# Moving the last dense product of a streaming encoder among the gathered expert rows

## The chip, the cores and the metric

One core of a Trainium2 chip runs the whole kernel. The metric is the device time of one execution in microseconds, as the median of several runs. Everything is float32.

## The reference, cut to what matters

One layer of a streaming encoder works on 576 tokens (512 of a prompt, 64 of a sample) of width 2048. A token mixer comes first, then the PEER channel mixer: each token picks 128 experts out of 16,384; row `u[idx]` of each gives a dot product with the token, and row `v[idx]` is added to the token with a weight made from it. The last step is the one that is changed here:

```python
h = h + _peer(_rmsnorm(h, g_ffn), ...)
e = _rmsnorm(h, g_ple)
h = h + jax.nn.sigmoid(e @ w_ple_gate) * (p @ w_ple_proj)
y = _rmsnorm(h, g_final)
```

`w_ple_gate` is 2048x2048, `w_ple_proj` is 256x2048.

## The kernel before

Tokens are five blocks of 128: blocks 0 to 3 are the prompt, block 4 (`SB`) holds the 64 sample tokens twice, each half with half of the experts. Blocks 0, 3 and 4 get their experts by gathers, one row of 128x2048 numbers (1 MB, one expert for each of 128 tokens) at a time; blocks 1 and 2 (`DENSE`) get only the `u` rows so, and their `v` part by a dense product of 32 steps (`NVG`), each with 4 MB of `peer_v` tiles. There are 576 `u` rows (`NROWS`); the `v` rows of a block follow their `u` rows 12 rows later (`LAG`). Rows 512 to 575 belong to block 4.

GpSimd issues the gathers into a ring of slots, six of them at the end (three for `u`, three for `v`), each when VectorE has used the slot's last row. VectorE works a `u` row at L2282 (`dots`) and a `v` row at L2294. ScalarE applies a GELU once in eight `u` rows (L1752, after rows 535, 543, 551, 559, 567, 575), and VectorE multiplies it with the gate before the first `v` row of those eight.

The embedding stage (`pe_embed`, `act_embed`, `dve_embed`) does the last step for blocks 1, 2, 3 and 0 (`EMBEDS[0]`, four blocks). First the blocks are turned: a quarter of a block is four 128x128 transposes on TensorE (L834) into one PSUM bank, which ScalarE copies with the gain (L842). ScalarE squares each block (L1320), VectorE and ScalarE make 1/rms of it (L848, L1323, L851; `dve_rs`, `act_rs`). Then come four groups of 512 columns (`DG`); in each, TensorE multiplies the four blocks with a 4 MB piece of `w_ple_gate`, loaded as four quarters (L1242, SyncE issues at L667), and with a piece of `w_ple_proj` (L1250); ScalarE takes the sigmoid (L1681); VectorE takes the result in two steps, `sigmoid * proj` (L2192) and the addition to h (L2196). Block 0 has been kept in memory (`h_scratch`) and is read back at L712, after the last dense step. The embedding of block 4 itself (`pe_last`, L1267 to L1296, and `sp_last`, which loads `w_ple_gate` once more as 16 rows of 1 MB, `w_row`) follows when all its rows are added, and then the final norm.

Each engine runs its instructions in one fixed order. It is written down as a key: every program yields numbers on a common scale, whose unit is one `u` row, and `braid` merges the programs by them. A `v` row has the key of the `u` row before it plus 0.5. So `EMBED_AT = (533, 1.05)` puts the turned copies of ScalarE at 534.05 to 535.0 and the four norms at 535.3 to 537, and `GROUP_ROWS = (538, 11.9)` puts what VectorE and ScalarE do for group i at 538 + 11.9 i. Equal keys go to the gathered rows first. TensorE and SyncE do these stages in plain program order.

Of the kernel before, what the change touches and what calls it, by code (L numbers as in the profile page):

```python
# [10 lines left out]
ALU = mybir.AluOpType  # L11
ACT = mybir.ActivationFunctionType
# [3 lines left out]
D = 2048  # L16
# [5 lines left out]
EPS = 1e-6  # L22
# [54 lines left out]
DENSE_AT = (404.6, 4.0)  # L77
GROUP_ROWS = (538, 11.9)

# [278 lines left out]
def build(nc, a, out):  # L358
    with ExitStack() as ctx:
# [159 lines left out]
        pT = late[:, 2 * D - NB * PLE:2 * D].rearrange("p (k t) -> p k t", k=PK)  # L519
        sig = late[:, 0:D].rearrange("p (i c) -> p i c", i=4)  # L520

        def hrow(t):

            return X[:, 4 * D:5 * D] if t == 0 else hslot(t)
        Wf = W[:, :, :].rearrange("p k c -> p (k c)")
# [8 lines left out]
        h2, sig2 = hslot(SB)[:, 0:2 * CG], hslot(SB)[:, 2 * CG:4 * CG]  # L534
        gf2 = late[:, 0:2 * CG]

# [42 lines left out]
        def ncol(i, c):  # L579
            return stat[:, 4 * i + c:4 * i + c + 1]  # L580

        def rs_of(what, g, j):
# [124 lines left out]
        def sp_embed(sp):  # L707
            sp.wait_ge(d_done, 4 * (NVG - 1))
            load_w(sp, a["w_ple_gate"][0], "ple", 0, range(0, 1))
            sp.wait_ge(d_done, 4 * NVG)  # L710
            sp.wait_ge(h_kept, 16)
            sp.dma_start(hrow(0), h_keep).then_inc(h_in, 16)  # L712
            for k in range(PK):
                sp.dma_start(wp[:, k, :], a["w_ple_proj"][0, k * P:(k + 1) * P, :]).then_inc(wp_in, 16)
            load_w(sp, a["w_ple_gate"][0], "ple", 0, range(1, DG))

        def sp_last(sp):

            for k in range(KT):
                if k < WQ - 1:  # L720
                    sp.wait_ge(used[k], prod.use0["ple", 0] + DG)
                elif k == WQ - 1:
                    sp.wait_ge(mm, prod.end("ple", 0))
                elif k == WQ:
                    sp.wait_ge(v_used, v_rows(NROWS) - 6)
                    sp.dma_start(cx[:, :], a["g_final"].rearrange("(o d) -> o d", o=1).to_broadcast([P, D])).then_inc(gf_in, 16)
                elif 6 <= k < 12:
                    _, what, x = ends[k - 6]
                    if what == "u":
                        sp.wait_ge(u_used, x + 1)  # L730
                    else:
                        sp.wait_ge(v_used, v_rows(x) + 1)
                elif k >= 12:
                    sp.wait_ge(row_used, k - 11)
                sp.dma_start(w_row(k), a["w_ple_gate"][0, k * P:(k + 1) * P, :]).then_inc(row_landed(k)[0], 16)
            sp.wait_ge(y_ready, y0 + 1)
            sp.dma_start(every_second(out["y_sample"][0], 0), halves(h2)[0].rearrange("p (a c) -> p a c", c=CG)).then_inc(y_out, 16)
# [15 lines left out]
        def sp_dense(sp):  # L753
# [12 lines left out]
            for m in range(NVG):  # L766
                if m * VT % CHUNK == 0:
                    c = m * VT // CHUNK
                    if c >= 2:
                        sp.wait_ge(d_done, 4 * (m - 2))  # L770
                    sp.dma_start(a_chunk(c).rearrange("p t k -> p (t k)"), a_keep[c].rearrange("i t k -> i (t k)")
                                 ).then_inc(chunk_in[c % 2], 16)
                if m == NVG - 4:
                    sp.wait_ge(picked[SB], PAIRS)
                    load_p(sp)
                if m >= 2:
                    sp.wait_ge(d_done, 4 * (m - 1))
                if m:
                    load_tiles(sp, m)

        def sync(sp):
# [55 lines left out]
        def act_turned(act, what, g, q, j, n, gain, src_bank):  # L837
# [5 lines left out]
            ins.then_inc(n_cp, 1)  # L843

        def dve_rs(dve, i, at, x):
            yield at(x)
            dve.wait_ge(n_sq, i + 1)
            dve.tensor_scalar(ncol(i, 1), ncol(i, 0), 1.0 / D, EPS, ALU.mult, ALU.add).then_inc(n_ms, 1)  # L848
            yield at(x + 0.1)
            dve.wait_ge(n_rt, i + 1)  # L850
            dve.reciprocal(ncol(i, 3), ncol(i, 2)).then_inc(n_rs, 1)  # L851
# [367 lines left out]
        def pe_embed(pe):  # L1219
            ts, n = EMBEDS[0], len(EMBEDS[0])  # L1220
            pe.wait_ge(d_add, 4 * NVG)
            for q in range(4):
                for j, t in enumerate(ts):
                    x = q * n + j
                    if x >= 6:
                        pe.wait_ge(n_cp, counts.quarter0["ple", 0] + x - 5)
                    if q == 0 and t == 3:
                        pe.wait_ge(v_used, v_rows(ROW0[SB]))
                    if q == 0 and t == 0:
                        pe.wait_ge(h_in, 16)  # L1230
                    pe_turn(pe, "ple", 0, q, j, n, hrow(t), x % 6)
            pe.wait_ge(n_cp, counts.quarters("ple", 0))
            pe.wait_ge(p_c, 2)
            for i in range(DG):
                U = prod.use0["ple", 0] + i
                for q in range(WQ):
                    pe.wait_ge(landed[q], 16 * (U + 1))
                    for j in range(n):
                        if q == 0 and i:
                            pe.wait_ge(e_sig, (i - 1) * n + j + 1)  # L1240
                        for k in range(q * KQ, (q + 1) * KQ):
                            ins = pe.matmul(bank(j), aT(k, j), W[:, k, :], start=(k == 0), stop=(k == KT - 1))  # L1242
# [10 lines left out]
                    if q < WQ - 1:  # L1253
                        ins.then_inc(used[q], 1)

        def pe_last(pe):
# [61 lines left out]
        def act_rs(act, i, src, junk, at, x):  # L1318
            yield at(x)
            act.activation(junk, src, ACT.Square, accum_out=ncol(i, 0)).then_inc(n_sq, 1)  # L1320
            yield at(x + 0.05)
            act.wait_ge(n_ms, i + 1)
            act.activation(ncol(i, 2), ncol(i, 1), ACT.Sqrt).then_inc(n_rt, 1)  # L1323
# [334 lines left out]
        def act_embed(act):  # L1658
# [4 lines left out]
            for q in range(4):  # L1663
                for j in range(n):
                    yield at(1 + 0.3 * q)
                    act_turned(act, "ple", 0, q, j, n, 2, (q * n + j) % 6)
            for j, t in enumerate(ts):
                i = counts.stat["ple", 0, j]
                if j:
                    act.wait_ge(n_sq, i)  # L1670
                yield from act_rs(act, i, hrow(t), late[:, 0:D], at, 2.2 + 0.5 * j)
            for i in range(DG):
                for j in range(n):
                    x = i * n + j
                    yield group_at(i, 0.3 * j)
                    act.wait_ge(mm, prod.mm0["ple", 0] + x + 1)
                    if i == 0:
                        act.wait_ge(n_rs, counts.stat["ple", 0, j] + 1)
                    if x >= 4:
# [3 lines left out]
        def act_last(act):  # L1683

            i, junk = counts.stat["ple", 1, 0], psum[:, 2:6, :].rearrange("p b c -> p (b c)")
            ts, squares = EMBEDS[0], late[:, 0:D]
            yield last_at(0)
# [29 lines left out]
            for s in range(2):  # L1717
                yield last_at(5 + s)
                act.wait_ge(n_rs, i + 1)
                act.wait_ge(mm, prod.end("ple", 0) + s + 1)  # L1720
# [458 lines left out]
        def dve_embed(dve):  # L2179
            ts, n = EMBEDS[0], len(EMBEDS[0])  # L2180

            def at(x):
                return embed_at(0, x)
            for j in range(n):
                yield from dve_rs(dve, counts.stat["ple", 0, j], at, 2.22 + 0.5 * j)
            for i in range(DG):
# [145 lines left out]
```

## Time and profile before

| | |
|---|---|
| time, median of 3 runs | 3743.24 us (3733.95 to 3745.58) |
| profiled execution, first to last instruction (span) | 3741.8 us; its time outside the span is not recorded, and the median is 1.4 us above the span |
| TensorE busy | 3104.3 us, 83% |
| VectorE busy | 2756.7 us, 74% |
| GpSimd busy | 1354.3 us, 36% |
| ScalarE busy | 624.2 us, 17% |
| DMA over the span | 388 GB/s mean; 417 to 422 GB/s in most slices |
| slice 37 of 40 (about 3368 to 3461 us) | 206 GB/s |
| chain that ended last | DMA 45%, VectorE 17%, TensorE 12% |

The busy shares are means over stages with different limits, so they say little about one stage. The change touches the last tenth of the span, and the views of that stretch are the ones to read.

### The profile page before, as it was taken

What the parts mean: (1) busy time and instruction counts of PE and PEld (TensorE: products, weight loads), DVE (VectorE), ACT (ScalarE), POOL (GpSimd) and SP (SyncE); (2) the same over time, 40 slices, a digit from 0 to 9 for tenths busy, and PEclk for the clock granted to TensorE, in tenths of its full rate; (3) what the DMA queues carried; (4) which work ended last, traced back from release to release, by engine and by line L of the source; (5) the groups of instructions that cost most, each with busy time, mean ns of one, the idle gap of its engine ahead of it and who ended that gap; (6) DMA issues with size and microseconds to landing.
All of it is one profiled execution on the core that took longest, in us unless ns stands there. A gap on an engine that the chain in (4) does not pass through costs nothing.

```text
span 3741.8 us, 26599 instructions
## 1 busy us (share of the span) xinstructions
PE 3104.3 (83%) x9234; PEld 1897.2 (51%) x9234; DVE 2756.7 (74%) x3844; ACT 624.2 (17%) x1601; POOL 1354.3 (36%) x908
## 2 busy tenths in 40 slices
PE   8998697999977299998886444999889999869974
PEld 4447343544456144554366433766666666644432
DVE  1014988677677899878768888888788998774885
ACT  2211110132011121123121556000000000002012
POOL 0001543325235453323335432334333433352662
PEclk9999798999988599999898556999999999989997
DMA  8889999999999999999999999999999999995998
GB/s 267 280 278 328 419 417 418 418 418 419 417 412 405 357 418 417 417 418 380 395 405 413 348 361 336 422 421 422 422 421 421 419 422 399 404 418 206 414 420 342
DMA packets 310262, 1453.01 MB, mean 388 GB/s; under 512 B 25776, under 2 KB 64112, under 8 KB 172016
## 3 DMA queue, kind: packets, MB, share of 16 engines
q0 software_dynamic: 129840, 944.83, 61.7%
q1 hardware_dynamic: 170112, 493.78, 34.6%
q10 hardware_dynamic: 10176, 12.70, 0.9%
q8 instruction: 73, 1.20, 0.1%
q14 instruction: 61, 0.50, 0.0%
HBM read 1424.48 MB, written 26.74 MB: 388 GB/s over the span
## 4 chain that ended last, share of the span: by engine, by line
DMA 45%; DVE 17%; PE 12%; POOL 6%; issue 6%; ACT 2%; SPq 0%; DVEq 0%; POOLq 0%; ACTq 0%
DMA ring<-in_peer_v,eidx 18%; DMA ring<-in_peer_u,eidx 17%; DVE ring L2282 7%; POOL ring L827 6%; PE psum L891 6%; DMA W<-in_w_peer_q 5%; DVE arena L2294 3%; DMA W<-in_w_out 2%; PE psum L1242 2%; PE psum L1154 1%; DMA a_scratch<-arena 1%; PE psum L1204 1%; DMA a_scratch<-W 1%; DMA arena<-h_scratch 1%; PE psum L1287 1%
## 5 line engine op out<-in xcount | busy, mean ns | idle before, releaser
L2282 DVE CUSTOM_DVE_ANT_0 ring<-ring,cx 128x2048 f32<-128x2048 f32 x576 | 1313.8, 2286 | 256.4 <-DMA ring<-in_peer_u,eidx 254.1
L827 POOL DMA_INDIRECT ring<-in_peer_u,eidx x576 | 868.9, 1509 | 1635.5 <-DVE dots L2282 1210.5
L2294 DVE SCALAR_TENSOR_TENSOR arena<-ring,wts,arena 128x2048 f32<-128x2048 f32 x320 | 751.7, 2349 | 210.6 <-DMA ring<-in_peer_v,eidx 192.4
L891 PE MATMUL psum<-W,actT 128*128 128x512 f32 x1792 | 797.4, 604 | 46.7 <-ACT actT L842 21.8
L827 POOL DMA_INDIRECT ring<-in_peer_v,eidx x320 | 480.3, 1501 | 665.9 <-DVE arena L2294 619.7
L891 PEld LDWEIGHTS psum<-W,actT 128*128 128x128 f32 x1792 | 343.9, 194 | 467.1 <-issue 450.6
L1154 PE MATMUL psum<-actT,W 128*128 128x128 f32 (+2 forms) x1536 | 294.9, 358 | 90.1 <-DMA W<-in_w_peer_q 79.2
L1154 PEld LDWEIGHTS psum<-actT,W 128*128 128x128 f32 x1536 | 269.3, 212 | 114.8 <-DMA W<-in_w_peer_q 86.0
L1752 ACT ACTIVATE gel<-dots 128x8 f32<-128x8 f32 x72 | 15.6, 216 | 1630.0 <-DVE dots L2282 1630.0
L1204 PE MATMUL psum<-arena 128*128 128x512 f32 x512 | 236.3, 619 | 38.4 <-DVE arena L2177 38.4
L1204 PE MATMUL psum<-arena,actT 128*128 128x512 f32 x512 | 233.2, 612 | 27.7 <-DVE arena L2177 27.5
L891 PE MATMUL psum<-W,arena 128*128 128x512 f32 x512 | 227.6, 606 | 23.9 <-DMA W<-in_w_out 23.6
L1204 PE MATMUL psum<-W,actT 128*128 128x512 f32 x512 | 225.4, 600 | 19.4 <-DMA actT<-a_scratch 16.1
L1204 PE MATMUL psum<-W,arena 128*128 128x512 f32 x512 | 225.8, 601 | 9.3 <-DVE arena L2177 9.1
L1204 PEld LDWEIGHTS psum<-arena 128*128 128x128 f32 x512 | 159.5, 316 | 114.6 <-DVE arena L2177 47.1
L1204 PEld LDWEIGHTS psum<-arena,actT 128*128 128x128 f32 x512 | 159.3, 315 | 100.3 <-DVE arena L2177 32.2
L1204 PEld LDWEIGHTS psum<-W,actT 128*128 128x128 f32 x512 | 159.9, 314 | 83.6 <-issue 20.5
L869 PE MATMUL psum<-W,actT 128*128 128x512 f32 x448 | 197.5, 600 | 0.0
L1204 PEld LDWEIGHTS psum<-W,arena 128*128 128x128 f32 x512 | 159.8, 314 | 74.3 <-DVE arena L2177 10.5
L891 PEld LDWEIGHTS psum<-W,arena 128*128 128x128 f32 x512 | 98.6, 195 | 148.8 <-issue 118.7
L2177 DVE TENSOR_TENSOR arena<-psum,arena 128x1024 f32<-128x1024 f32 x128 | 155.7, 1217 | 0.0
L869 PEld LDWEIGHTS psum<-W,actT 128*128 128x128 f32 x448 | 85.3, 193 | 102.3 <-issue 102.0
(317 smaller groups left out, 2558.0 us busy)
## 6 DMA issues: line engine op xcount, KB each, us to landing
W<-in_w_in SPq DMA_DIRECT2D x168, 1024.0 KB, 12.4
W<-in_peer_v SPq DMA_DIRECT2D x64, 1024.0 KB, 15.8
arena<-in_peer_v SPq DMA_DIRECT2D x64, 1024.0 KB, 17.9
W<-in_w_out SPq DMA_DIRECT2D x48, 1024.0 KB, 17.4
W<-in_w_peer_q SPq DMA_DIRECT2D x48, 1024.0 KB, 24.2
W<-in_w_ple_gate SPq DMA_DIRECT2D x24, 1024.0 KB, 14.8
ring<-in_peer_u,eidx POOLq DMA_INDIRECT x576, 17.4
a_scratch<-W SPq DMA_DIRECT2D x8, 1024.0 KB, 14.4
```

The source lines that it names most:

```text
L827: pool.indirect_dma_start(ring[:, slot, :], None, a["peer_u" if what == "u" else "peer_v"][0], off(ix, 0)).then_inc(ring_in[slot], 16)
L869: ins = pe.matmul(bank(4 * s + j), lhs(k, j), W[:, k, :], start=(k == 0), stop=(k == KT - 1))
L891: ins = pe.matmul(bank(4 * s + j), lhs(at_k, j), w_pair(q)[:, k, s * CG:(s + 1) * CG], start=(at_k == 0), stop=(at_k == KT - 1))
L1154: ins = pe.matmul(bank(2 * (i % 2) + c // 2)[:, at:at + fresh], W[:, k, c * P:(c + 1) * P], actT[:, k, 0:fresh], start=(k == 0 and c % 2 = ...
L1204: ins = pe.matmul(bank(at % 3 * 2 + half), a_chunk(c)[:, i // 2 * P:(i // 2 + 1) * P, m * VT % CHUNK + x], v_tiles(m)[:, x, c0:c0 + 512], ...
L1242: ins = pe.matmul(bank(j), aT(k, j), W[:, k, :], start=(k == 0), stop=(k == KT - 1))
L1287: ins = pe.matmul(psum[SAMPLE * b:SAMPLE * (b + 1), s, :], actT[:, k, 0:SAMPLE], w_row(k)[:, cols_of(s, b)], start=(k == 0), stop=(k == KT ...
L1752: act.activation(gel[:, n % DEEP, :], dots[:, n % DEEP, :], ACT.Gelu).then_inc(gelud, 1)
L2177: dve.tensor_tensor(hc, psum[:, at % 3 * 2:at % 3 * 2 + 2, :], hc, ALU.add).then_inc(d_add, 1)
L2282: dve.tensor_tensor_reduce(row, row, cx[:, :], 1.0, 0.0, ALU.mult, ALU.add, dots[:, n % DEEP, c:c + 1]).then_inc(u_used, 1)
L2294: dve.scalar_tensor_tensor(out=hslot(t), in0=ring[:, slot, :], scalar=wts[:, n % DEEP, c:c + 1], in1=hslot(t), op0=ALU.mult, op1=ALU.add). ...
```

## The change

The squares of the four blocks are taken as soon as each block's last quarter is copied, and the four means, roots and reciprocals become one instruction each on 128x4 numbers (`embed_cols`), at key 541.5 (`EMBED_RS`). `rooted` adapts the counts of the semaphores to that. The keys of the groups go from 538, 549.9, 561.8, 573.7 to 548.5, 559, 569.5, 580; there is no gathered row above 575.5. Block 0 of h is read back by SyncE behind the tiles of the last dense step, into half of ring slots 6 and 7 (`late`), and the sigmoids and the squares go to the place (`spare`) where it was before. TensorE turns the first two quarters, does quarter 0 of group 0's product, turns quarter 2, does quarter 1 of the product, turns quarter 3, and goes on; turning uses banks 4 to 7 (four instead of six). In `sp_last` the load of `g_final` into `cx` moves from row 4, where it waited for all but six `v` rows, to row 6, where it waits for the last `u` row.

```diff
-GROUP_ROWS = (538, 11.9)
+GROUP_ROWS = (548.5, 10.5)
+EMBED_RS = 541.5
...
-        sig = late[:, 0:D].rearrange("p (i c) -> p i c", i=4)
+        spare = X[:, 4 * D:5 * D]
+        sig = spare.rearrange("p (i c) -> p i c", i=4)
         def hrow(t):
-            return X[:, 4 * D:5 * D] if t == 0 else hslot(t)
+            return late[:, 0:D] if t == 0 else hslot(t)
...
+        def embed_cols(c):
+            i = counts.stat["ple", 0, 0]
+            return stat[:, 4 * i:4 * (i + len(EMBEDS[0]))].rearrange("p (f c) -> p f c", c=4)[:, :, c]
...
             load_w(sp, a["w_ple_gate"][0], "ple", 0, range(0, 1))
             sp.wait_ge(d_done, 4 * NVG)
-            sp.wait_ge(h_kept, 16)
-            sp.dma_start(hrow(0), h_keep).then_inc(h_in, 16)
...
-                elif k == WQ:
-                    sp.wait_ge(v_used, v_rows(NROWS) - 6)
+                elif k == 6:
+                    sp.wait_ge(u_used, NROWS)
                     sp.dma_start(cx[:, :], a["g_final"]...)
-                elif 6 <= k < 12:
+                if 6 <= k < 12:
...
                 if m:
                     load_tiles(sp, m)
+                if m == NVG - 1:
+                    sp.wait_ge(p_t, 2)
+                    sp.wait_ge(h_kept, 16)
+                    sp.dma_start(hrow(0), h_keep).then_inc(h_in, 16)
...
+        def rooted(i):
+            return min(i, counts.stat["ple", 0, 0]) + 1 + (1 if i >= counts.stat["ple", 1, 0] else 0)
...
         def pe_embed(pe):
             ts, n = EMBEDS[0], len(EMBEDS[0])
-            pe.wait_ge(d_add, 4 * NVG)
-            for q in range(4):
+            def turn(q):
                 for j, t in enumerate(ts):
                     x = q * n + j
-                    if x >= 6:
-                        pe.wait_ge(n_cp, counts.quarter0["ple", 0] + x - 5)
+                    if x >= 4:
+                        pe.wait_ge(n_cp, counts.quarter0["ple", 0] + x - 3)
...
-                    pe_turn(pe, "ple", 0, q, j, n, hrow(t), x % 6)
-            pe.wait_ge(n_cp, counts.quarters("ple", 0))
+                    pe_turn(pe, "ple", 0, q, j, n, hrow(t), 4 + x % 4)
+            pe.wait_ge(d_add, 4 * NVG)
             pe.wait_ge(p_c, 2)
+            turn(0)
+            turn(1)
             for i in range(DG):
...
+                        if i == 0:
+                            pe.wait_ge(n_cp, counts.quarter0["ple", 0] + q * n + j + 1)
                         for k in range(q * KQ, (q + 1) * KQ):
...
+                    if i == 0 and q + 2 < 4:
+                        turn(q + 2)
...
         def act_embed(act):
             for q in range(4):
-                for j in range(n):
+                for j, t in enumerate(ts):
                     yield at(1 + 0.3 * q)
-                    act_turned(act, "ple", 0, q, j, n, 2, (q * n + j) % 6)
-            for j, t in enumerate(ts):
-                i = counts.stat["ple", 0, j]
-                if j:
-                    act.wait_ge(n_sq, i)
-                yield from act_rs(act, i, hrow(t), late[:, 0:D], at, 2.2 + 0.5 * j)
+                    act_turned(act, "ple", 0, q, j, n, 2, 4 + (q * n + j) % 4)
+                    if q < 3:
+                        continue
+                    i = counts.stat["ple", 0, j]
+                    if j:
+                        act.wait_ge(n_sq, i)
+                    act.activation(spare, hrow(t), ACT.Square, accum_out=ncol(i, 0)).then_inc(n_sq, 1)
+            yield EMBED_RS
+            act.wait_ge(n_ms, rooted(counts.stat["ple", 0, 0]))
+            act.activation(embed_cols(2), embed_cols(1), ACT.Sqrt).then_inc(n_rt, 1)
...
         def dve_embed(dve):
-            for j in range(n):
-                yield from dve_rs(dve, counts.stat["ple", 0, j], at, 2.22 + 0.5 * j)
+            yield EMBED_RS
+            dve.wait_ge(n_sq, counts.stat["ple", 0, n - 1] + 1)
+            dve.tensor_scalar(embed_cols(1), embed_cols(0), 1.0 / D, EPS, ALU.mult, ALU.add).then_inc(n_ms, 1)
+            yield EMBED_RS + 0.6
+            dve.wait_ge(n_rt, rooted(counts.stat["ple", 0, 0]))
+            dve.reciprocal(embed_cols(3), embed_cols(2)).then_inc(n_rs, 1)
```

## Rows read from the trace of the kernel before

**Rows 1.** Windows of the last stretch: busy time by engine, clock, DMA share.

```profile
core 0: us, PE busy (x) PEld busy (x) DVE busy (x) ACT busy (x) POOL busy (x), PEclk, DMA share, GB/s
3355.00:3380.00 25.00, 9.25 (x54) 7.67 (x55) 0.00 (x0) 14.75 (x54) 0.94 (x1) 0.70 0.79 328
3355.00:3450.00 95.00, 79.25 (x212) 38.52 (x213) 29.23 (x33) 28.59 (x72) 15.00 (x10) 0.90 0.56 219
...
3450.00:3657.00 207.00, 178.90 (x417) 78.99 (x415) 176.10 (x132) 16.56 (x22) 132.07 (x71) 0.94 1.01 413
```

**Rows 2.** Timeline of VectorE: start, length, line, operation, idle time before.

```profile
3352.70 2.29 DVE L2282 CUSTOM_DVE_ANT_0 ring<-ring,cx 128x2048 f32<-128x2048 f32 x1 [0.93 <-DMA ring<-in_peer_u,eidx]
...
3380.78 0.15 DVE L848 TENSOR_SCALAR stat<-stat 128x1 f32<-128x1 f32 x1 [25.78 <-ACT ring L1320]
...
3428.15 0.69 DVE L2192 TENSOR_TENSOR ring<-psum,ring 128x512 f32<-128x512 f32 x1 [31.10 <-PE psum L1250]
...
3689.26 2.35 DVE L2294 SCALAR_TENSOR_TENSOR arena<-ring,wts,arena 128x2048 f32<-128x2048 f32 x1 [2.83 <-DMA ring<-in_peer_v,eidx]
```

**Rows 3.** Timeline of TensorE from the first turn to the last product.

```profile
3339.90 2.82 PE L834 MATMUL psum<-misc,arena 128*128 128x128 f32 x12 [6.24 <-DVE arena L2177]
3364.10 6.09 PE L834 MATMUL psum<-misc,arena 128*128 128x128 f32 x40 [21.38 <-DMA arena<-h_scratch]
...
3378.81 9.75 PE L1242 MATMUL psum<-W,actT 128*128 128x512 f32 x16 [5.53 <-ACT arena L842]
...
3443.33 7.03 PE L1242 MATMUL psum<-W,actT 128*128 128x512 f32 x16
...
3627.01 1.88 PE L1250 MATMUL psum<-arena,ring 128*128 128x512 f32 x4
```

**Rows 4.** Timeline of ScalarE: turned copies, square, GELU, table load, sigmoid.

```profile
3366.26 2.19 ACT L842 ACTIVATE actT<-psum,gT 128x128 f32<-128x128 f32 x8
...
3378.33 2.33 ACT L1320 ACTIVATE ring<-arena 128x2048 f32<-128x2048 f32 x1
...
3463.15 0.21 ACT L1752 ACTIVATE gel<-dots 128x8 f32<-128x8 f32 x1 [19.35 <-DVE dots L2282]
...
3559.23 0.21 ACT L1752 ACTIVATE gel<-dots 128x8 f32<-128x8 f32 x1 [45.42 <-DVE dots L2282]
3559.46 1.28 ACT L1681 ACT_TABLE_LOAD   x1
3560.75 1.84 ACT L1681 ACTIVATE ring<-psum,stat 128x512 f32<-128x512 f32 x3
...
3657.17 0.21 ACT L1752 ACTIVATE gel<-dots 128x8 f32<-128x8 f32 x1 [27.96 <-DVE dots L2282]
```

**Rows 5.** DMA queues: packets, MB, share; 3306 to 3355 us.

```profile
q0 software_dynamic: 2229, 16.21, 80.1%
q1 hardware_dynamic: 2013, 4.02, 21.7%
```

**Rows 6.** The loads of w_ple_gate at line 667.

```profile
L667 SPq DMA_DIRECT2D W<-in_w_ple_gate x16: 367/368/9768, 3306.2 to 3565.4; - x16
...
DMA to landing us min/median/max: 5.0/16.2/51.3
```

**Rows 7.** Timeline of TensorE, and its clock, after the last gathered row.

```profile
3681.66 5.03 PE L1267 MATMUL psum<-arena,ring 128*64 128x512 f32 x16 [52.77 <-DVE arena L2294]
3691.66 7.09 PE L1272 MATMUL psum<-misc,arena 128*128 128x64 f32 x32 [4.97 <-DVE arena L2294]
3698.68 8.49 PE L1287 MATMUL psum<-W,actT 128*64 128x512 f32 x32
...
3724.51 7.04 PE L1287 MATMUL psum<-W,actT 128*64 128x512 f32 x32
...
3692.00:3696.00 4.00, 4.00 (x21) 4.00 (x20) 0.00 (x0) 1.55 (x8) 0.00 (x0) 0.50 1.01 420
```

**Rows 8.** Timeline of ScalarE's DMA queue: the writes of y_prompt.

```profile
3718.40 7.13 ACTq L1716 DMA_DIRECT2D out_y_prompt<-arena  x4
```

More of the change, by code:

```diff
@@ L534, in build @@
         h2, sig2 = hslot(SB)[:, 0:2 * CG], hslot(SB)[:, 2 * CG:4 * CG]
-        gf2 = late[:, 0:2 * CG]
+        gf2 = spare[:, 0:2 * CG]
         ends = ring_ends()
@@ L732, in sp_last @@
                         sp.wait_ge(v_used, v_rows(x) + 1)
-                elif k >= 12:
+                if k >= 12:
                     sp.wait_ge(row_used, k - 11)
@@ L849, in dve_rs @@
             yield at(x + 0.1)
-            dve.wait_ge(n_rt, i + 1)
+            dve.wait_ge(n_rt, rooted(i))
             dve.reciprocal(ncol(i, 3), ncol(i, 2)).then_inc(n_rs, 1)
@@ L1321, in act_rs @@
             yield at(x + 0.05)
-            act.wait_ge(n_ms, i + 1)
+            act.wait_ge(n_ms, rooted(i))
             act.activation(ncol(i, 2), ncol(i, 1), ACT.Sqrt).then_inc(n_rt, 1)
@@ L1676, in act_embed @@
                     act.wait_ge(mm, prod.mm0["ple", 0] + x + 1)
-                    if i == 0:
-                        act.wait_ge(n_rs, counts.stat["ple", 0, j] + 1)
+                    if x == 0:
+                        act.wait_ge(n_rs, rooted(counts.stat["ple", 0, 0]))
                     if x >= 4:
@@ L1685, in act_last @@
             i, junk = counts.stat["ple", 1, 0], psum[:, 2:6, :].rearrange("p b c -> p (b c)")
-            ts, squares = EMBEDS[0], late[:, 0:D]
+            ts, squares = EMBEDS[0], spare
             yield last_at(0)
@@ L1718, in act_last @@
                 yield last_at(5 + s)
-                act.wait_ge(n_rs, i + 1)
+                act.wait_ge(n_rs, rooted(i))
                 act.wait_ge(mm, prod.end("ple", 0) + s + 1)
```

## The prediction

> **What bounds the kernel now.** I read the page first, for which stretch is ill: in nearly every slice DMA is full and slice 37 falls to 206 GB/s. Then windows around it [rows 1]: from 3450 to 3657 us DMA is 100% busy at 413 GB/s while VectorE is busy 176 of 207 us, so the gathered rows are bound by DMA there. From 3355 to 3450 DMA moves only 219 GB/s. At the 413 of the later window, the same bytes take 50 us: 45 us of the 95 are lost. VectorE's timeline [rows 2] tells why. It ends u row 535 at 3355.0 and waits 25.8 us, until 3380.8, in the first of the four norms at key 535.3; a few rows later it waits 31.1 us more, until 3428.2, for group 0's results at key 538.1. Nothing behind may pass, so no slot is freed and GpSimd issues no gather. What holds it: block 0 is asked for only at the end of the dense product, so TensorE, which starts to turn at 3339.9, halts until 3364.1 for its landing (21.4 us of idle time are put down to it) and starts the product at 3378.8 [rows 3]. The end is set by the gathers: last v row at 3689.3 [rows 2], then the tail of block 4, 3691.7 to 3741.8 [rows 7]. TensorE has finished its product at 3628.9 [rows 3] and waits 52.8 us [rows 7]. So a product begun earlier is worth nothing by itself; rows going on are.
>
> **The read of block 0.** It moves one SyncE issue ahead of group 0's four weight quarters, behind the last tiles. It is 1 of some 115 MB that pass anyway, so no bytes are added. From 3306 to 3355 the hardware queue got 4.02 MB beside 16.21 MB of gathers [rows 5], 82 GB/s; the first quarters were issued from 3306.2 and the longest took 51.3 us [rows 6]. If block 0 runs ahead of them in full they are up to 12 us later, if it is in before they start, 0. I take 0 to 3, since it is issued some 30 us earlier. The quarters are then in at about 3321, 3333, 3345 and 3358 (four equal shares of that time), before TensorE asks. A stall of 21 us goes from TensorE.
>
> **Turning beside the product.** ScalarE takes 1.03 us per turned quarter of a block (eight copies in 2.06 us from start to start) [rows 4], so eight of them from 3341 are done by 3349.3. TensorE starts the product when the last of them is turned, 3346.5. A group takes 61.7 us: (3628.9 - 3443.3)/3 [rows 3]. Group 0 adds 2.7 us for the slow clock at its start (9.75 against 7.03 us for 16 matmuls) and two turnings of 16 transposes at 0.15 us (40 in 6.09 [rows 3]), 4.9. Group 0 ends at 3346.5 + 61.7 + 2.7 + 4.9 = 3415.8 instead of 3443.3, group 1 at 3477.5.
>
> **The norms.** A quarter of a group's product is 32 records in the trace, 13.7 us. Quarter 3 is turned behind quarter 1 of the product: from 3346.5 + 2.7 + 13.7 + 2.4 + 13.7 = 3379.0. ScalarE then does four copies and four squares, 1.03 + 2.08 us each [rows 4] (the accumulator read is in the second), and ends at 3392. What is queued behind it on ScalarE is the GELU of rows 528 to 535, since the turned copies have keys below 535; and VectorE needs that GELU before the v row of key 540.5. Rows pace: from the GELU of row 543 to that of row 575, 32 rows took 3657.2 - 3463.2 = 194.0 us [rows 4], 6.06 us a row, 48.5 per eight. So VectorE comes to 540.5 at 3355 + 5 x 6.06 = 3385 and waits 7 us. The gathers have six slots of 2.5 us each (1.05 MB at 413 GB/s) underway, so DMA has work for some 12 us and this costs nothing; past that it costs one for one, and VectorE catches up, with 4.6 us of work a row [rows 2]. One-step norms themselves save VectorE and ScalarE some small instructions, 1 us at most, off the path: 0.
>
> **Taking the results 10 rows later.** Key 548.5 comes at 3355 + 13.5 x 6.06 = 3437, when all of group 0 is there. VectorE's 8 operations of 0.69 us run beside DMA. What is late next: ScalarE's sigmoids of group 1 have key 559, a tie that the gathered rows win, so they stand behind the GELU of row 559. Before, that GELU already held group 2's sigmoids back: they follow it and a table load at 3560.75, three at once [rows 4]. Now row 559 comes at 3355 + 3 x 48.5 = 3500.5, while TensorE has done group 1 at 3477.5 and may not write group 2 before those sigmoids. The first is there at 3500.5 + 0.2 + 1.3 + 0.6 = 3502.6; TensorE has stood 25 us. Its clock falls to the lower level in such a pause, as in rows 3, so 2.7 us more. Group 2 ends at 3502.6 + 2.7 + 61.7 = 3567.0, group 3 at 3628.7: as late as before. Row 567 comes at 3549, the first result of group 2 at 3551, so nothing waits there.
>
> On the table load the Trainium skill's page "ScalarE: Activation LUTs", section "What ACT_TABLE_LOAD costs", says something else than the row: a switch costs 1.28 us of load and 1.38 of drain, 2.66 together. Here the sigmoid starts 0.01 us behind the 1.28 us load [rows 4]. By the page the start of group 2 and the end would come 1.4 us later.
>
> **The end of the gathers.** Rows 560 to 575 take another 2 x 48.5 us by pace, until 3597. By tiles it is less, as only group 3's weights run beside them: 36 tiles of 2.53, 3592. Then 13 v rows are left. They took 34.5 us before (3657.2 to 3691.6) with up to ten tiles for the tail beside them; at VectorE's 2.35 us each, 31. Last v row at 3623 to 3628. Then come group 3's results, key 580: 5.5 us for eight operations, but the last needs the product's end, 3628.7 + 0.7. Both give about 3631.
>
> **The tail.** It now starts with L1267, which must follow group 3's results and took 5.03 us in the old gap; L1272 7.09 and the first L1287 8.49 us followed [rows 7]. They ran at clock 0.50, the lower level; TensorE now comes from a running product. The last 32 of L1287 take 7.04 at full clock [rows 7]. L1267 has 16 of the same shape, 3.5, and L1272 at half its time 3.6. So L1272 starts at 3634.5 and the rest is 50.1 - 3.5 - 1.4 = 45.2 us: 3679.6. Against that gain, only three of the 16 weight rows come before group 3's end: 13 and g_final are 14 x 2.53 = 35 us from 3629, in at 3667 with 2 us to land, just when TensorE wants the last (3668). The four writes of y_prompt, 4 MB before from 3718.4 [rows 8], now fall among them and take up to 10 us. Bounds 0 and 10; I take 3. Sum: 3679.6 + 3.4 = 3683 against 3741.8, and against the median, which is 1.4 above the span, 3684.4: 59 us less. Check: 45 us of DMA are refilled and 13 tiles (33 us) move behind the gathers, which would end 65 us earlier; the tail, TensorE's group 3 and the takes return some.
>
> **Rivals.** *TensorE bounds throughout.* If rows go faster than 6.06 us, to VectorE's 4.6, row 559 is there before 3477.5, group 3 ends at 3601, and the gathers with their takes decide: 3620 + 8 + 45 = 3673. For: at 219 GB/s there were holes to be filled; against: DMA is full whenever rows flow [rows 1]. Chance 0.15. *Holes stay.* If block 0 or the weights come late, VectorE's wait at 540.5 exceeds 12 us, and each us more moves row 559 and all behind it. The hardware queue's 82 GB/s beside full gathers [rows 5] brings a weight quarter in 12.8 us where TensorE uses one in 13.7, so there is little to spare. One quarter late by its own 12.8 us, with the y_prompt writes at their 10 instead of 3, gives 3684 + 13 + 7 = 3704; two late, 3717. Against: from 3450 on both queues ran full and TensorE lost nothing. Chance 0.2. *Slower than before.* One mechanism: the turned copies of quarters 2 and 3 stand ahead of the GELU of row 535 in ScalarE's order, and behind the product in TensorE's. If quarter 1 of the weights were not in, VectorE would stand at 540.5. It decides from the point where that lasts 12 + 59 = 71 us, that is TensorE's turning of quarter 3 at 3443 instead of 3379. The quarter's landing at 3333, against 3363 when it is wanted, speaks against it: time 3760, chance 0.03. *No change* (the reread still holds TensorE to 3364, holes merely change places): 3740, chance 0.02.
>
> **Numbers.** Likeliest, row 559 starts group 2: 0.6, 3684. The range 3666 to 3712 takes in the TensorE rival and most of the holes'. A difference under 0.3% (11 us) can't be told from none. Faster 0.95, within 0.02, slower 0.03.
>
> **What the profile after should show.** VectorE without a wait over 10 us from 3340 to 3620; DMA above 400 GB/s from 3355 on; product from about 3347; a TensorE gap of some 25 us before group 2, ended by a sigmoid (L1681's line) that follows a GELU; group 3's end near 3629; the gathers' last v row before it; L1267 directly behind. I am wrong if TensorE has no such gap (then 3673), if VectorE stands long at key 540.5 or 541.5, or if the tail takes over 55 us because its weight rows arrive late.

## The result, and the profile after

The changed kernel takes 3695.61 us (median of 4 runs, 3685.42 to 3703.6) against 3743.41 us: ratio 0.9873, 95% interval 0.9851 to 0.9894, so 47.8 us less where 59 were forecast. The profiled execution has a span of 3701.7 us and its own time is 3703.45, 1.8 above it.

Windows of the changed kernel, with the columns of [rows 1]:

```profile
core 0: us, PE busy (x) PEld busy (x) DVE busy (x) ACT busy (x) POOL busy (x), PEclk, DMA share, GB/s
3355.00:3380.00 25.00, 24.62 (x79) 12.35 (x78) 15.64 (x11) 9.54 (x37) 14.35 (x8) 1.00 1.02 418
3355.00:3450.00 95.00, 94.62 (x254) 44.27 (x253) 70.67 (x50) 29.40 (x72) 52.54 (x31) 1.00 1.02 416
3607.00:3646.00 39.00, 32.92 (x77) 14.25 (x75) 31.71 (x17) 4.24 (x6) 14.97 (x9) 0.98 1.01 422
```

From 3355 to 3450 us DMA is full at 416 GB/s instead of 219, and VectorE is busy 70.7 us instead of 29.2. Both holes of [rows 2] are gone: from 3340 to 3620 us VectorE's longest wait is 2.7 us.

TensorE's timeline, to be read beside [rows 3] and [rows 7]. L842 is the old L834, L1258 the old L1242, L1266 the old L1250, L1285, L1290 and L1305 the old L1267, L1272 and L1287:

```profile
3350.80 2.82 PE L842 MATMUL psum<-misc,arena 128*128 128x128 f32 x12 [11.03 <-DVE arena L2199]
...
3356.73 7.03 PE L1258 MATMUL psum<-W,actT 128*128 128x512 f32 x16
...
3422.03 7.03 PE L1258 MATMUL psum<-W,actT 128*128 128x512 f32 x16
...
3482.11 1.88 PE L1266 MATMUL psum<-arena,ring 128*128 128x512 f32 x4
3513.89 9.30 PE L1258 MATMUL psum<-W,actT 128*128 128x512 f32 x16 [29.90 <-ACT arena L1703]
...
3638.05 1.88 PE L1266 MATMUL psum<-arena,ring 128*128 128x512 f32 x4
3650.38 5.85 PE L1285 MATMUL psum<-arena,ring 128*64 128x512 f32 x16 [10.46 <-issue]
3656.16 3.79 PE L1290 MATMUL psum<-misc,arena 128*128 128x64 f32 x32
3659.88 7.09 PE L1305 MATMUL psum<-W,actT 128*64 128x512 f32 x32
```

ScalarE's timeline, beside [rows 4] (L1774 is the GELU, L1703 the sigmoid):

```profile
3398.17 0.30 ACT L1774 ACTIVATE gel<-dots 128x8 f32<-128x8 f32 x1
...
3511.54 0.21 ACT L1774 ACTIVATE gel<-dots 128x8 f32<-128x8 f32 x1 [44.54 <-DVE dots L2308]
3511.76 1.28 ACT L1703 ACT_TABLE_LOAD   x1
3513.06 2.42 ACT L1703 ACTIVATE arena<-psum,stat 128x512 f32<-128x512 f32 x4
...
3607.77 0.21 ACT L1774 ACTIVATE gel<-dots 128x8 f32<-128x8 f32 x1 [29.34 <-DVE dots L2308]
```

VectorE's timeline at the end of the gathers (L2320 is the `v` row, L2218 and L2222 take results):

```profile
3630.29 12.30 DVE L2320 SCALAR_TENSOR_TENSOR arena<-ring,wts,arena 128x2048 f32<-128x2048 f32 x5 [0.45 <-DMA ring<-in_peer_v,eidx]
3643.34 2.35 DVE L2320 SCALAR_TENSOR_TENSOR arena<-ring,wts,arena 128x2048 f32<-128x2048 f32 x1 [0.75 <-DMA ring<-in_peer_v,eidx]
3645.61 0.68 DVE L2218 TENSOR_TENSOR arena<-psum,arena 128x512 f32<-128x512 f32 x1
...
3650.31 0.69 DVE L2222 TENSOR_TENSOR ring<-ring,arena 128x512 f32<-128x512 f32 x1
```

The reader is to see four things. The first turned quarter waited for the last dense addition, not for block 0, and the product began 6.0 us behind that addition. TensorE pauses once within the product, 29.9 us before group 2, and it ends just behind a sigmoid that follows the GELU of row 559. The product ends at 3639.9 us. The last `v` row ends at 3645.7, later than the product, and only behind it come the eight operations on group 3's results; L1285 starts at 3650.4.

One thing must be known before the two traces are compared. The last dense addition ends at 3339.84 us in the profiled execution of before and at 3350.74 in this one, though the instructions up to there are the same but for the one read. In the twelve experiments below it ended anywhere from 3324.8 to 3348.7. So I count from there, to the end of the span. That stretch is 402.0 us before and 351.0 after: 51.0 us less, against 58.8 by the forecast's own marks (3339.8 to 3683).

| mark, us from the last dense addition | forecast | measured |
|---|---|---|
| product starts | 6.7 | 6.0 |
| group 0 ends | 76.0 | 71.5 |
| group 1 ends | 137.7 | 133.3 |
| group 2 starts | 162.8 | 163.2 |
| group 3 ends | 288.9 | 289.2 |
| last GELU, of row 575 | 252 to 257 | 257.0 |
| last `v` row | 283 to 288 | 295.0 |
| L1272's successor (L1290) starts | 294.7 | 305.4 |
| from there to the end | 48.5 | 45.5 |
| end | 343.2 | 351.0 |

### The profile page after: what moved, and what is told of

Read it like the earlier page. It is cut to its first block, busy times and chain, and to the rows that moved or that the text cites. A ratio compares the mean times of both kernels' runs of the same rounds, so it can differ in the third digit from the quotient of the medians.

```text
span 3701.7 us, 26591 instructions
## 1 busy us (share of the span) xinstructions
PE 3100.8 (84%) x9234; PEld 1889.5 (51%) x9234; DVE 2757.5 (74%) x3838; ACT 622.3 (17%) x1598; POOL 1338.8 (36%) x908
## 4 chain that ended last, share of the span: by engine, by line
DMA 44%; DVE 15%; PE 13%; POOL 6%; issue 6%; ACT 2%; SPq 0%; DVEq 0%; ACTq 0%
DMA ring<-in_peer_u,eidx 18%; DMA ring<-in_peer_v,eidx 17%; DVE ring L2308 7%; POOL ring L835 6%; PE psum L903 6%; DMA W<-in_w_peer_q 5%; PE psum L1258 3%; DVE arena L2320 3%; DMA W<-in_w_out 2%; DMA a_scratch<-arena 2%; PE psum L1166 1%; DMA a_scratch<-W 1%; DVE W L2182 1%; PE psum L1305 1%; ACT arena L1639 1%
## 5 line engine op out<-in xcount | busy, mean ns | idle before, releaser
L2320 DVE SCALAR_TENSOR_TENSOR arena<-ring,wts,arena 128x2048 f32<-128x2048 f32 x320 | 751.9, 2350 | 219.9 <-DMA ring<-in_peer_v,eidx 204.2
L903 PE MATMUL psum<-W,actT 128*128 128x512 f32 x1792 | 801.2, 606 | 47.3 <-ACT actT L850 22.9
L835 POOL DMA_INDIRECT ring<-in_peer_v,eidx x320 | 464.2, 1451 | 606.4 <-DVE arena L2320 559.0
L903 PEld LDWEIGHTS psum<-W,actT 128*128 128x128 f32 x1792 | 344.8, 195 | 470.9 <-issue 452.4
L1166 PE MATMUL psum<-actT,W 128*128 128x128 f32 (+2 forms) x1536 | 295.0, 358 | 93.1 <-DMA W<-in_w_peer_q 81.8
L1774 ACT ACTIVATE gel<-dots 128x8 f32<-128x8 f32 x72 | 15.3, 212 | 1651.7 <-DVE dots L2308 1651.6
L1216 PE MATMUL psum<-W,actT 128*128 128x512 f32 x512 | 225.9, 601 | 31.3 <-DMA actT<-a_scratch 28.2
L1216 PEld LDWEIGHTS psum<-W,actT 128*128 128x128 f32 x512 | 159.8, 314 | 96.2 <-issue 33.1
L881 PE MATMUL psum<-W,actT 128*128 128x512 f32 x448 | 197.3, 599 | 0.0
L1258 PE MATMUL psum<-W,actT 128*128 128x512 f32 x256 | 115.4, 602 | 29.9 <-ACT arena L1703 29.9
```

What stands on the lines that cost most here:

```text
L835: pool.indirect_dma_start(ring[:, slot, :], None, a["peer_u" if what == "u" else "peer_v"][0], off(ix, 0)).then_inc(ring_in[slot], 16)
L881: ins = pe.matmul(bank(4 * s + j), lhs(k, j), W[:, k, :], start=(k == 0), stop=(k == KT - 1))
L903: ins = pe.matmul(bank(4 * s + j), lhs(at_k, j), w_pair(q)[:, k, s * CG:(s + 1) * CG], start=(at_k == 0), stop=(at_k == KT - 1))
L1166: ins = pe.matmul(bank(2 * (i % 2) + c // 2)[:, at:at + fresh], W[:, k, c * P:(c + 1) * P], actT[:, k, 0:fresh], start=(k == 0 and c % 2 = ...
L1216: ins = pe.matmul(bank(at % 3 * 2 + half), a_chunk(c)[:, i // 2 * P:(i // 2 + 1) * P, m * VT % CHUNK + x], v_tiles(m)[:, x, c0:c0 + 512], ...
L2320: dve.scalar_tensor_tensor(out=hslot(t), in0=ring[:, slot, :], scalar=wts[:, n % DEEP, c:c + 1], in1=hslot(t), op0=ALU.mult, op1=ALU.add). ...
```

## The experiments

Each was timed in 4 runs, together with the kernel before, and its ratio is to the runs of before that were taken with it (medians from 3737.8 to 3744.1). The stretch is counted as above, in the profiled execution. "Tail" runs from the end of the last `v` row to the end of the span. The gain over the kernel before in the stretch and the gain in the median agree within 5 us in every kernel but e7, where they are 10 us apart.

| kernel | median us | ratio, 95% interval | stretch | last `v` row | tail |
|---|---|---|---|---|---|
| before | 3743.41 | 1 | 402.0 | 351.8 | 50.2 |
| changed | 3695.61 | 0.9873 (0.9851 to 0.9894) | 351.0 | 295.0 | 56.0 |
| e1 early takes | 3715.91 | 0.9935 (0.991 to 0.996) | 377.0 | 326.5 | 50.5 |
| e2 late takes only | 3705.07 | 0.9897 (0.9874 to 0.9921) | 365.8 | 310.3 | 55.4 |
| e3 late read | 3706.04 | 0.9905 (0.9883 to 0.9927) | 364.0 | 308.5 | 55.5 |
| e4 turn all first | 3697.67 | 0.988 (0.9859 to 0.9902) | 351.4 | 296.1 | 55.3 |
| e5 keys ahead of GELU | 3699.81 | 0.9895 (0.9869 to 0.9921) | 363.4 | 307.3 | 56.0 |
| e6 hold rows 4 to 15 | 3692.58 | 0.9876 (0.985 to 0.9901) | 350.7 | 295.3 | 55.4 |
| e7 four norms | 3698.93 | 0.989 (0.9871 to 0.9909) | 350.7 | 295.3 | 55.4 |
| e8 combined | 3692.89 | 0.987 (0.9851 to 0.9889) | 351.9 | 296.7 | 55.2 |
| e9 hold all rows | 3691.84 | 0.9876 (0.984 to 0.9912) | 350.7 | 295.1 | 55.5 |
| e10 combined, rows earlier | 3693.8 | 0.9872 (0.9848 to 0.9896) | 350.9 | 299.5 | 51.4 |
| e11 combined, hold all | 3686.73 | 0.9848 (0.9822 to 0.9875) | 343.8 | 292.9 | 51.0 |
| e12 hold all to the last | 3693.14 | 0.9879 (0.9847 to 0.991) | 354.1 | 287.1 | 67.0 |

**Where the gain comes from: e1 to e4.**

e1, on the changed kernel:

```diff
-GROUP_ROWS = (548.5, 10.5)
-EMBED_RS = 541.5
+GROUP_ROWS = (538, 11.9)
+EMBED_RS = 536.9
```

> The changed kernel with the group keys of before (538, 11.9) and the one-step norms at key 536.9; early read, new places and turning beside the product stay. I count from the last dense addition to the end of the span: 402.0 us before, 351.0 changed. Theory (the gain is that VectorE stays off instructions that TensorE has not served yet): VectorE comes to 536.9 some 12 us before the squares are done and to 538.1 before group 0's first result, which is there 56 us after the last dense addition; it stands in the norm and then at most of the four results, some 40 us in all, of which about 12 are hidden by gathers underway. 370 to 385 us, with DMA idle. Rival (the early read alone brings the gain): 350 to 357 us.

377.0 us, in the theory's range: 26 of the 51 us are lost again with block 0 read early and everything else in place. VectorE's timeline of e1 (L2208 is the norm, L2218 takes a result):

```profile
3381.12 0.17 DVE L2208 TENSOR_SCALAR stat<-stat 128x4 f32<-128x4 f32 x1 [20.68 <-ACT arena L1690]
...
3389.57 0.69 DVE L2218 TENSOR_TENSOR arena<-psum,arena 128x512 f32<-128x512 f32 x1 [1.53 <-PE psum L1266]
...
3394.72 0.69 DVE L2218 TENSOR_TENSOR arena<-psum,arena 128x512 f32<-128x512 f32 x1 [3.73 <-PE psum L1266]
...
3405.02 0.69 DVE L2218 TENSOR_TENSOR arena<-psum,arena 128x512 f32<-128x512 f32 x1 [1.52 <-PE psum L1266]
```

It stands 20.7 us in the norm and then up to 3.7 us at each of the four results, 8.4 us together; TensorE delivers them 5.15 us apart. These 29.1 us are less than the 40 that I expected.

e2, on the kernel before:

```diff
-GROUP_ROWS = (538, 11.9)
+GROUP_ROWS = (548.5, 10.5)
```

> The kernel before with only the group keys of the change (548.5, 10.5). Theory: the second hole (31 us at group 0's results) goes, the first (26 us in the norm behind the read of block 0) stays. Row 559 then comes about 175 us after the last dense addition, group 2 starts there and 126 us of product and 55 to 60 of tail follow: 358 to 368 us from the last dense addition, against 402.0 before and 351.0 changed. Rival (the read of block 0 is the first cause, the keys a detail): 385 to 402 us.

365.8 us, in the theory's range: this one line brings 36 of the 51 us. It takes away more than the 31.1 us of the second hole: before, VectorE waited at each of group 0's four results, 38.0 us in all. The first hole is still there on VectorE, and TensorE's pause before group 2 has appeared:

```profile
3373.41 0.15 DVE L848 TENSOR_SCALAR stat<-stat 128x1 f32<-128x1 f32 x1 [23.12 <-ACT ring L1320]
```

```profile
3514.70 10.12 PE L1242 MATMUL psum<-W,actT 128*128 128x512 f32 x16 [16.44 <-ACT ring L1681]
```

e3, on the changed kernel:

```diff
                 if m:
                     load_tiles(sp, m)
-                if m == NVG - 1:
-                    sp.wait_ge(p_t, 2)
-                    sp.wait_ge(h_kept, 16)
-                    sp.dma_start(hrow(0), h_keep).then_inc(h_in, 16)
...
             sp.wait_ge(d_done, 4 * NVG)
+            sp.wait_ge(p_t, 2)
+            sp.wait_ge(h_kept, 16)
+            sp.dma_start(hrow(0), h_keep).then_inc(h_in, 16)
             for k in range(PK):
```

> The changed kernel with block 0 read back only after the last dense step, as before, to its new place. Theory: the product starts some 20 us later, so quarter 3 is turned and squared some 20 us later, and VectorE stands at key 540.5 for the GELU that ScalarE has behind the turned copies, about 30 us, of which 12 are hidden: 362 to 375 us from the last dense addition. Rival (the norms' late key already covers the read, so its early issue is worth nothing): 349 to 354 us.

364.0 us, in the theory's range. VectorE's wait is where the theory put it, at the product of GELU and gate (L2313) ahead of the `v` row of key 540.5, and it is shorter than I expected, 20.5 us instead of about 30:

```profile
3396.72 0.17 DVE L2313 TENSOR_TENSOR wts<-gel,gate 128x8 f32<-128x8 f32 x1 [20.54 <-ACT gel L1773]
```

A wait of 20.5 us cost 13.0 in the stretch, so some 7.5 us of it were covered, fewer than the 12 that I had for gathers underway.

e4, on the changed kernel:

```diff
             turn(0)
             turn(1)
+            turn(2)
+            turn(3)
...
-                    if i == 0 and q + 2 < 4:
-                        turn(q + 2)
```

> The changed kernel with all four quarters turned ahead of the product. Theory: group 0 ends some 10 us later, which the 30 us that TensorE stands before group 2 absorb; the squares are done earlier. No change: 348 to 354 us from the last dense addition. Rival (TensorE's start sets the end): 360 to 363 us.

351.4 us: no change. The product begins 14.3 us behind the last dense addition instead of 6.0, and the pause before group 2 shrinks from 29.9 to 25.1 us. TensorE's timeline of e4, first matmuls of groups 0 and 2:

```profile
3357.24 7.03 PE L1260 MATMUL psum<-W,actT 128*128 128x512 f32 x16
```

```profile
3506.10 9.16 PE L1260 MATMUL psum<-W,actT 128*128 128x512 f32 x16 [25.10 <-ACT arena L1703]
```

So starting the product behind two turned quarters is worth nothing here.

**The one-step norms: e7**, on the changed kernel:

```diff
-            act.activation(embed_cols(2), embed_cols(1), ACT.Sqrt).then_inc(n_rt, 1)
+            for j in range(n):
+                yield EMBED_RS + 0.1 * j
+                i = counts.stat["ple", 0, j]
+                act.wait_ge(n_ms, i + 1)
+                act.activation(ncol(i, 2), ncol(i, 1), ACT.Sqrt).then_inc(n_rt, 1)
...
```

VectorE's means and reciprocals are split in the same way.

> The changed kernel with the four norms made separately again, at the late key 541.5: four instructions of 128x1 in place of each of 128x4 on VectorE and ScalarE. Theory: the one-step form is worth nothing by itself, since VectorE has 1.5 us a row to spare; 350 to 353 us from the last dense addition. Rival (each separate step costs a wait on the other engine in VectorE's order): 355 to 360.

350.7 us in the stretch: nothing lost. The form of the norms doesn't matter. Their key does: at 536.9 (e1) VectorE stood 20.7 us in them. No run moves that key alone. The median of e7, 3698.93 us, is 3.3 above the changed kernel's, and the intervals of the two ratios overlap.

**Does TensorE's pause set the end? e5**, on the changed kernel:

```diff
-GROUP_ROWS = (548.5, 10.5)
+GROUP_ROWS = (547, 9.5)
```

> The changed kernel with the group keys at 547, 556.5, 566, 575.5: each group's sigmoids stand ahead of the GELU of rows 559, 567 and 575 in ScalarE's order. Theory (TensorE's 30 us pause before group 2 is set by that GELU, but DMA sets the end): no pause at group 2, group 3 waits for the GELU of row 559's successor at most some us, the product ends 15 to 30 us earlier, and the 13 late weight rows then compete with the last v rows. The last v row comes at 295 to 305 us from the last dense addition and the end at 348 to 360, against 351.0: no gain. Rival (the pause sets the end, as I had it in the forecast): the end comes as much earlier as the product, 325 to 340.

There is no pause before group 2 any more, the product ends 257.4 us from the last dense addition instead of 289.2, and yet the stretch is 363.4 us, 12 longer, a little beyond my range. The idea of the forecast, that the pause sets the end together with the gathers, falls. But e5 changes two things at once: SyncE issues weight row 3 and those behind it when the product ends, so these loads come earlier too. The hardware queue moved 8.6 MB from the last GELU to the last `v` row; in the changed kernel it was 4.2 MB, half of it after row 3 was issued at 3638.2 us. The last 13 `v` rows of e5 come 5 us apart while weight rows run beside them. VectorE's timeline of e5:

```profile
3604.36 2.35 DVE L2320 SCALAR_TENSOR_TENSOR arena<-ring,wts,arena 128x2048 f32<-128x2048 f32 x1 [2.62 <-DMA ring<-in_peer_v,eidx]
3609.32 2.35 DVE L2320 SCALAR_TENSOR_TENSOR arena<-ring,wts,arena 128x2048 f32<-128x2048 f32 x1 [2.61 <-DMA ring<-in_peer_v,eidx]
3614.29 2.35 DVE L2320 SCALAR_TENSOR_TENSOR arena<-ring,wts,arena 128x2048 f32<-128x2048 f32 x1 [2.62 <-DMA ring<-in_peer_v,eidx]
...
3617.45 12.22 DVE L2320 SCALAR_TENSOR_TENSOR arena<-ring,wts,arena 128x2048 f32<-128x2048 f32 x5 [0.74 <-DMA ring<-in_peer_v,eidx]
...
3641.01 2.35 DVE L2320 SCALAR_TENSOR_TENSOR arena<-ring,wts,arena 128x2048 f32<-128x2048 f32 x1 [2.61 <-DMA ring<-in_peer_v,eidx]
```

**What makes the last v rows slow: e6, e9, e12.** They differ from the changed kernel by one wait of SyncE in `sp_last`. This is e9; e12 has 1 in place of 6:

```diff
             for k in range(KT):
+                if k == 0:
+                    sp.wait_ge(v_used, v_rows(NROWS) - 6)
                 if k < WQ - 1:
```

e6 has the wait for all but one ahead of row 4.

> The changed kernel; SyncE waits ahead of weight row 4 until all v rows but one are used, so rows 4 to 15 and g_final no longer compete with the last gathers. Theory: the last v row comes 4 to 8 us earlier (287 to 291 us from the last dense addition instead of 295.0), and the rows still come in time for the tail of 56 us: 343 to 348 us in all. Rival (the tail then waits for its rows): 351 to 360.

A miss: the last `v` row stays at 295.3 us. The wait held the rows back by some 5 us only, when nearly all gathers had landed, since row 3 ahead of them waits for the product's end anyway. Rows 1 and 2 still ran beside the gathers.

> The changed kernel; SyncE waits ahead of weight row 0 until all v rows but six are used, so none of the 16 rows shares DMA with most of the last 13 v rows. After the last u row these took 37.9 us in the changed kernel and 38.2 in e6, where rows 0 to 3 still ran beside them. Theory (the v rows' own tiles at 2.5 us each, 33 us, plus two or three weight rows at 2.5 us make the 38 us): 31 to 34 us from the last u row to the last v row, the last v row at 288 to 291 us from the last dense addition, the tail 56 us, all in all 344 to 347. Rival (VectorE or the issue of the gathers sets these 38 us): 37 to 39 us, and 350 to 353 in all.

Another miss: the last `v` row comes 39.8 us behind the last GELU, and 350.7 in all lies in the rival's range. But the timeline of VectorE shows the mechanism:

```profile
3580.37 12.30 DVE L2322 SCALAR_TENSOR_TENSOR arena<-ring,wts,arena 128x2048 f32<-128x2048 f32 x5 [0.19 <-DMA ring<-in_peer_v,eidx]
...
3592.85 9.74 DVE L2322 SCALAR_TENSOR_TENSOR arena<-ring,wts,arena 128x2048 f32<-128x2048 f32 x4
...
3608.94 2.35 DVE L2322 SCALAR_TENSOR_TENSOR arena<-ring,wts,arena 128x2048 f32<-128x2048 f32 x1 [2.62 <-DMA ring<-in_peer_v,eidx]
3613.89 2.35 DVE L2322 SCALAR_TENSOR_TENSOR arena<-ring,wts,arena 128x2048 f32<-128x2048 f32 x1 [2.61 <-DMA ring<-in_peer_v,eidx]
```

Nine `v` rows come in 2.46 us each. SyncE's rows are released at 3597.7, and the next three `v` rows start 5 us apart, the last one 3.7 us behind them. I had put the release too early: what was gained before it was lost behind it.

> As e9, but the hold ahead of weight row 0 lasts until all v rows but one are used, so that no weight row at all shares DMA with the last v rows. In e9 the first v rows after the hold began came at 2.5 us each and the last four at 5.0, 3.7 to 5.0 beside the released rows. Theory (DMA shared with weight rows makes the 38 us): the last v row 30 to 34 us after the last u row, 287 to 291 us from the last dense addition. Then 17 tiles of 2.5 us, 43 us, must come within the 43 us after which TensorE wants the last of them, with 4 MB of y_prompt written among them: the tail is 56 to 63 us, 345 to 352 in all. Rival (VectorE or the issue of the gathers): 37 us or more from the last u row, whatever the rows do.

Now all 13 `v` rows come without a gap and the last one is 32.3 us behind the last `u` row's GELU (287.1 us in the stretch), where the changed kernel needs 37.9:

```profile
3591.00 12.29 DVE L2322 SCALAR_TENSOR_TENSOR arena<-ring,wts,arena 128x2048 f32<-128x2048 f32 x5 [0.19 <-DMA ring<-in_peer_v,eidx]
...
3603.48 19.65 DVE L2322 SCALAR_TENSOR_TENSOR arena<-ring,wts,arena 128x2048 f32<-128x2048 f32 x8
3623.05 0.69 DVE L2220 TENSOR_TENSOR arena<-psum,arena 128x512 f32<-128x512 f32 x1
```

That settles the cause: the weight rows beside the gathers made the difference of 5.6 us. It brings no time, since the rows must come afterwards. TensorE's timeline of e12, with L1287 the old L1267 and L1307 the old L1287:

```profile
3627.82 3.65 PE L1287 MATMUL psum<-arena,ring 128*64 128x512 f32 x16 [3.04 <-issue]
...
3666.12 3.12 PE L1307 MATMUL psum<-W,actT 128*64 128x512 f32 x8 [2.88 <-DMA W<-in_w_ple_gate]
3671.02 3.68 PE L1307 MATMUL psum<-W,actT 128*64 128x512 f32 x8 [1.79 <-DMA W<-in_w_ple_gate]
```

It waits 7.5 us in all for its last four weight rows; the tail is 67.0 us, 4 above my range, and the stretch 2 above it. L1287 takes 3.65 us behind a pause of 3 us, at a granted clock of 1.00; in the changed kernel L1285 took 5.85 behind 10.5 us, at a mean of 0.60 (3650 to 3656 us).

**A better order: e8, e10, e11.** All three have e5's keys and spread VectorE's last `v` rows, so that group 3's results are taken between them:

```diff
                 else:
-                    yield last + 0.5
+                    ends_at += last == NROWS - 1
+                    yield last + 0.5 + 0.5 * max(0, ends_at - 1)
```

In e8 SyncE holds row 4 until all `v` rows but one are used; in e10 until all but six; in e11 it holds row 0 until all but six.

> The changed kernel with the keys of e5, the hold of e6, and VectorE's keys of the last 12 v rows spread by 0.5, so that it takes group 3's results between them and not behind them. Theory: the last v row at 284 to 292 us from the last dense addition; the product of block 4 with w_ple_proj then lies ahead of that row, and the tail is 50 us as before the change instead of 56: 335 to 342 us. Rival (DMA work of the tail only moves, and the rows arrive late): 346 to 355.

No gain. The last `v` row came at 296.7, not at 284 to 292, and TensorE waits for its last weight rows, 6.7 us in all, as the rival had it (three of its waits in the timeline of e8):

```profile
3676.77 1.94 PE L1307 MATMUL psum<-W,actT 128*64 128x512 f32 x8 [1.28 <-DMA W<-in_w_ple_gate]
3681.69 2.44 PE L1307 MATMUL psum<-W,actT 128*64 128x512 f32 x8 [2.98 <-DMA W<-in_w_ple_gate]
3686.59 3.52 PE L1307 MATMUL psum<-W,actT 128*64 128x512 f32 x8 [2.46 <-DMA W<-in_w_ple_gate]
```

> e8 with the hold ahead of weight row 4 ending six v rows from the end instead of one, since in e8 TensorE waited 6.7 us in all for its last weight rows. Theory: the waits in the tail are gone (50 us from the last v row), the last v row stays at 296 to 299 us: 346 to 349 us. Rival (rows 4 to 15 now delay the v rows by as much as they come earlier): 351 to 354.

The waits are gone and the tail is 51.4 us, but the last `v` row moves to 299.5: the two cancel, 350.9, between the theory's range and the rival's.

> As e10, but the hold is ahead of weight row 0. Theory: after the last u row VectorE has 13 v rows and 8 takes, 36 us of work, so fewer weight rows beside the gathers gain at most 2 us at the last v row (293 to 297 us), and 13 rows and more come behind it: the tail is 50 to 54 us. 344 to 350 us. Rival (the rows are late as in e8): 352 to 357.

343.8 us, 7 less than the changed kernel, and the best median of all, 3686.73 us. It differs from e9 (350.7) only in the earlier keys and the spread `v` rows; which of these two brings the 7 us was not run. Its ratio to before, 0.9848, has an interval (0.9822 to 0.9875) that overlaps the changed kernel's, so by the medians alone it isn't certainly better; the stretch, of one execution, suggests that it is.

## Why the prediction was right, point by point

**The holes.** Right. VectorE stood in two waits and DMA ran dry, and both are gone. e2 gives 36 us for the late taking of the results, by one line; e1 shows that without the late keys 26 are lost. The rest of the gain needs the early read: without it (e3) 13 us are lost.

**The early read.** Right that it adds nothing and frees the first turn. It was issued at the last tiles, as said, and TensorE never waited for block 0 or for weights.

**Group 0 and the norms.** The product began where it was forecast. Group 0 ended 4.5 us earlier: the first 16 matmuls took 7.03 us at a granted clock of 1.00 (3355 to 3380 us), so the 2.7 us for the slow clock were not due, and the turned quarters took 1.7 us each instead of 2.4. The 7 us wait of VectorE at key 540.5 didn't come: the GELU ran at 3398.2 and VectorE ended `u` row 540 at 3399.7. That was close: 1.5 us. e3 shows that the dependence is real: of a wait of 20.5 us only 7.5 were covered, where I had 12. That the start of the product and the form of the norms don't matter is e4's and e7's result.

**Row 559 starts group 2.** Right as to when: 163.2 us against 162.8 by the forecast, group 3 done at 289.2 against 288.9. The pause was 29.9 us instead of 25, since group 1 ended earlier. The forecast took this chain as one that sets the end together with the gathers. That is not so: in the changed kernel the product ends 5.8 us ahead of the last `v` row, a product begun 8 us later lost nothing (e4), and without the pause the end came later, not earlier (e5). The gathers set the end, and TensorE had slack.

**The table load.** The sigmoid starts 0.02 us behind the end of the 1.28 us load. The figure of 2.66 us for a switch in the Trainium skill's page "ScalarE: Activation LUTs", section "What ACT_TABLE_LOAD costs", isn't seen in this place; the measurement decides.

**The step that was mis-sized** is the end of the gathers. I gave the last 13 `v` rows 31 us, at VectorE's 2.35 us each. They took 37.9. Each needs 2.5 us of DMA, 32.3 in all, as e12 shows with no other transfer beside them, and the other 5.6 are weight rows 1 and 2 in the same 16 engines: from the last GELU to 3638.2 us they moved 2.10 MB, 5.0 us at 422 GB/s. (Row 0 had passed before, and row 3 was issued at 3638.2.) A smaller slip lies ahead of it: my count of 36 tiles for rows 560 to 575 gave 252 for the last GELU, and my pace of rows 257; it came at 257.0. DMA was full there except around 3520 to 3535 us, behind group 1's results, where it moved 335 GB/s. So the last `v` row came at 295.0, 7 to 12 us late, and the operations on group 3's results moved fully behind it. L1285 starts 8.4 us late, and behind its pause it took 5.85 us instead of 3.5. Together L1290 starts 10.7 us late. Against that, 3.0 us came back: the y_prompt writes, for which I had 3 us, cost the tail nothing here (another 0.4 us in the forecast's sum has no stated source). 10.7 - 3.0 = 7.7, and the stretch is 7.8 over the forecast. That the total is nearer than L1290's start is luck: the second error happens to point the other way.

**The signs of being wrong.** The forecast named a tail of over 55 us as one of them. From the last `v` row it is 56.0, but not for the reason given: TensorE waited for no weight row in it. By that count the forecast's own marks give 55 to 60 us, so the sign says little. What made the tail longer than the 50.2 us of before is that L1290 starts 10.4 us behind the last `v` row, where before it started at once. And the last `v` row came behind the product's end, not before it, so L1285 did not follow directly.

**The rivals.** TensorE never bound the stretch. Holes did not stay. The turned copies did not hold VectorE. One part of the change has no run of its own, the load of `g_final` behind row 4. It can have had little effect: all but six `v` rows were used by 3629.8 us, ahead of row 3's issue at 3638.2, so the old wait would have been over.

## What to carry to other kernels

An engine that runs in a fixed order should meet an instruction only when its input is surely there: ten rows of slack in a key gave 36 of the 51 us of the whole change. When the stream behind such a wait is bound by DMA, starting the other engine earlier is worth only what keeps the stream running: a product begun 8 us later lost nothing (e4), and one without its pause cost 12 us (e5). Loads of the next stage that run beside the last gathers take DMA time from them (2.1 MB cost 5.6 us here), so hold them back as long as the next stage's engine can bear it; a wait a few rows too long (e12) or too short (e9) gave all of it back.

## What the runs showed that I had not expected

The last dense addition ended between 3324.8 and 3350.7 us in fourteen profiled executions of almost the same instructions, a spread of 26 us. The stretch behind it repeated within 0.7 us in five kernels (350.7, 350.7, 350.7, 351.0, 351.4), the changed one, e4, e6, e7 and e9. In three of the four experiments what was changed turned out not to matter; in e9 a gain and a loss cancel. Counting from a mark inside the trace told apart changes of a few us that the medians, with intervals of 0.2% to 0.4%, could not.

In e9 and e5, where both DMA queues had work, gathered rows came 5 us apart, twice the 2.5 us that they take alone. The bytes were shared evenly: from 3604 to 3614 us of e9 each queue moved 2.11 MB.
